# First layer of a four-layer trunk: shift and scale chunks in pairs, values in one pass over eight banks, the other modulation chunks dealt to attention, projection and FFN

## Chip, core and metric

One core of a Trainium2 chip runs the whole program once. The metric is the device time in microseconds, median of three runs.

## What is computed

```python
for li in range(DEPTH):                       # 4 layers: attention, retention, neighbourhood, attention
    sh1, sc1, gt1, sh2, sc2, gt2 = ada_mod(c, w_ada[li], b_ada[li])       # silu(c) @ w + b, 6 x 1024
    zsh1, zsc1, zgt1, zsh2, zsc2, zgt2 = ada_mod(cz, w_ada[li], b_ada[li])
    hx = modulate(x, norm_g[li, 0], sh1, sc1) # rms_norm(x, g) * (1 + scale) + shift
    hz = modulate(z, norm_g[li, 0], zsh1, zsc1)
    ox, oz = mixer(hx, hz, ...)               # layer 0: differential attention, 8 heads
    x = x + gt1 * ox
    x = x + gt2 * swiglu(modulate(x, norm_g[li, 1], sh2, sc2), ffn_in[li], ffn_out[li])
    # the same for z (the context) with its own modulation
return rms_norm(x, final_g)
```

x and ctx have 256 tokens of 1024 features each, all in f32. The FFN's hidden width is 2816.

## The kernel before

Features lie on the partitions: xT is 8 tiles (m or k) of 128 x 512 tokens, the first 256 columns x (stream 0), the others the context (stream 1). Each product of the layers is three matmuls of fp32r parts (h_hi w_hi, h_lo w_hi, h_hi w_lo). The weights are 424 blocks of 128x1024, called units; unit c goes through a ring of four slots: SyncE (SP) loads it to w_raw, ScalarE rounds it to w_hi (`conv`, in two halves), GpSimd subtracts to w_lo (two halves, `lo_ready`), TensorE uses it and counts `unit_used`. Each engine has one queue in program order, written out by hand; semaphores join them.

Modulation of a layer is 48 chunks of 128x1024 (shift 1, scale 1, gate 1, shift 2, scale 2, gate 2, eight each). For each chunk VectorE makes two products, one for each stream, with the conditioning vector: one SCALAR_TENSOR_TENSOR with an accumulated sum each (`ada_product`, L1452). `ada_sums` (L1460) adds the bias, `modulation` (L1492) makes the amplitude gain*(1+scale). `ada_done` counts finished chunks.

Layer 0 computes all its 48 chunks itself, with the conditioning in SBUF (cond_0): chunks 0 to 15 (`ada_first_group`, groups of four loaded as 2 MB) ahead of the first norm, 16 to 47 (`ada_rest_groups`) in `values`, between and behind the copies of the value product. Layers 1 to 3 have theirs computed in the FFN of the layer before, with the conditioning in PSUM (cond_p, in the high banks): 40 chunks in the loop over the hidden tiles, 8 behind it, from a ring of two chunks (ada_raw). TensorE starts the second half of the FFN output, which writes the high banks, when `ada_done` has all of them.

The norm: ScalarE squares x, VectorE adds the squares to ssum (`add_square`, L1520), TensorE multiplies with ones (`square_sum`), ScalarE makes rstd (`root`). For each tile VectorE scales (`scaled`, L1542), ScalarE adds the shift and rounds (`high`, h_hi), VectorE makes the rest (`low_part`, L1550, h_lo, counts `h_ready`). In layer 0 stream 0 is normalised wholly, then stream 1. The value product has 8 units, 4 token blocks and 2 feature halves; `values` runs over half 0 in banks 0 to 3, then over half 1 in banks 6, 7, 4, 5, and reads the second four units for half 1.

Attention has 8 tiles (one head pair each). In tile t TensorE makes q (bank 6) and k (bank 7), turns and weights tile t-1, then makes the scores of tile t. VectorE's queue of a tile: `weights_(t-1)`, rotate q (L1689), rotate k, two maxima (L1711), `subnorm(t-1)` (L1748), four maxima, `low(t-1)` (L1754). `project`: units 24 to 31; for tiles 0 to 4 VectorE adds the residual (L1501), ScalarE squares it (the conversion of the next unit stands ahead of each square in its queue), VectorE adds the square. Tiles 5 to 7 are done for x first, then for the context, which waits for the x residual of tile 5 (`x_new`).

## Time and profile before

| | us |
|---|---|
| median of 3 runs (2588.33 to 2590.04) | 2589.16 |
| profiled execution | 2592.92 |
| its span | 2591.1 |
| TensorE busy | 2421.3 |
| VectorE busy | 1289.2 |
| GpSimd busy | 1118.2 |
| ScalarE busy | 970.4 |

Times in the rows are microseconds from the start of the span. The page cuts the span in 40 slices of 64.8 us; a 9 is 90% busy or more. A timeline row gives the start, the length, the engine, the line, what is written and read, how many instructions it merges, and in brackets the idle time before it and the instruction that ended that.

### The profile page before, as it was taken

How to read it: one execution, taken by the hardware profiler on the slowest of the kernel's cores; microseconds unless marked ns; L12 is line 12 of the kernel's file. 1: busy time of each engine (PE TensorE's matmuls, PEld its weight loads, DVE VectorE, ACT ScalarE, POOL GpSimd, SP SyncE). 2: the span in 40 equal slices, each digit the busy share in tenths (PEclk: the TensorE clock that was granted, in tenths of full speed). 3: DMA queues.
4: the chain of work that ended last, by engine and by line, in shares of the span. 5: the costliest groups of instructions: out<-in, count | busy, mean ns of one | idle time of the engine just before them, and what ended most of it. 6: DMA issues, size and time to landing. Idle time of an engine off the chain costs nothing.

```text
span 2591.1 us, 37198 instructions
## 1 busy us (share of the span) xinstructions
PE 2421.3 (93%) x12212; PEld 1992.5 (77%) x12212; DVE 1289.2 (50%) x2275; ACT 970.4 (37%) x1943; POOL 1118.2 (43%) x855
## 2 busy tenths in 40 slices
PE   0729999999999999999999999999999999998998
PEld 0516678888887777788888887777888888777998
DVE  7996657654423333226666314554766443475211
ACT  2205544333223333323333224554432323455563
POOL 2321234444543433343544545223444554434896
PEclk9969999999999999999999999999999999999999
DMA  7256124554433222233655433231555442323554
GB/s 299 106 186 98 50 65 173 201 193 163 154 90 94 81 67 70 73 97 116 217 194 178 170 90 106 74 84 54 174 201 192 163 154 90 103 68 98 170 182 135
DMA packets 116466, 341.64 MB, mean 132 GB/s; under 512 B 34977, under 2 KB 36257, under 8 KB 115745
## 3 DMA queue, kind: packets, MB, share of 16 engines
q1 hardware_dynamic: 108352, 335.01, 39.4%
q10 hardware_dynamic: 8032, 5.52, 1.5%
q8 instruction: 55, 0.90, 0.1%
q14 instruction: 27, 0.21, 0.0%
HBM read 335.80 MB, written 4.69 MB: 131 GB/s over the span
## 4 chain that ended last, share of the span: by engine, by line
issue 60%; POOL 22%; PE 16%; DVE 1%; POOLq 1%; ACT 1%; DMA 0%; DVEq 0%; ACTq 0%; SPq 0%
POOL w_lo L492 22%; PE low_banks L499 15%; PE high_banks L499 1%; POOLq L491 0%; DVE tmp L1542 0%; POOLq L486 0%; DVE h_lo L1550 0%; ACT w_hi L1038 0%; DMA w_raw<-in_weights 0%; DMA ret_exp<-in_ret_exp 0%; DVE ssum_rstd L1452 0%; DVE xT L2028 0%; ACT lnm L1062 0%; POOLq L207 0%; ACT ssum_rstd L1063 0%
## 5 line engine op out<-in xcount | busy, mean ns | idle before, releaser
L492 POOL TENSOR_TENSOR w_lo<-w_raw,w_hi 128x512 fp32r<-128x512 f32 x848 | 1117.7, 1345 | 1454.2 <-ACT w_hi L1038 1453.5
L1038 ACT ACTIVATE w_hi<-w_raw 128x512 fp32r<-128x512 f32 x848 | 483.5, 624 | 474.1 <-PE low_banks L499 223.9
L499 PE MATMUL low_banks<-h_hi,w_hi 128*128 128x512 f32 (+1 forms) x1792 | 643.6, 359 | 14.8 <-POOL w_lo L492 7.7
L499 PE MATMUL low_banks<-h_lo,w_hi 128*128 128x512 f32 (+1 forms) x1792 | 634.5, 354 | 0.0
L499 PE MATMUL low_banks<-h_hi,w_lo 128*128 128x512 f32 (+1 forms) x1792 | 634.2, 354 | 0.0
L499 PEld LDWEIGHTS low_banks<-h_hi,w_hi 128*128 128x128 f32 x1792 | 340.5, 190 | 70.9 <-issue 11.3
L499 PEld LDWEIGHTS low_banks<-h_lo,w_hi 128*128 128x128 f32 x1792 | 340.7, 190 | 47.6 <-issue 1.9
L499 PEld LDWEIGHTS low_banks<-h_hi,w_lo 128*128 128x128 f32 x1792 | 340.6, 190 | 46.4
L1452 DVE SCALAR_TENSOR_TENSOR ssum_rstd<-ada_raw,high_banks 128x1024 f32<-128x1024 f32 x288 | 351.2, 1220 | 44.6 <-DMA ada_raw<-in_ada_w 36.9
L1360 ACT ACTIVATE lnm<-low_banks 128x512 f32<-128x512 f32 (+1 forms) x88 | 47.8, 544 | 427.3 <-PE low_banks L499 427.2
L1929 DVE TENSOR_TENSOR tmp<-low_banks,lnm 128x512 f32<-128x512 f32 (+1 forms) x88 | 55.0, 625 | 284.9 <-ACT lnm L1360 281.2
L499 PE MATMUL high_banks<-h_hi,w_hi 128*128 128x512 f32 (+1 forms) x384 | 148.4, 387 | 14.1 <-ACT v_all L1146 14.1
L499 PE MATMUL high_banks<-h_lo,w_hi 128*128 128x512 f32 (+1 forms) x384 | 144.5, 376 | 0.0
L499 PE MATMUL high_banks<-h_hi,w_lo 128*128 128x512 f32 (+1 forms) x384 | 144.4, 376 | 0.0
L499 PE MATMUL high_banks<-u_hi,w_hi 128*128 128x256 f32 (+1 forms) x424 | 141.0, 332 | 0.5 <-POOL w_lo L492 0.5
L499 PE MATMUL high_banks<-u_lo,w_hi 128*128 128x256 f32 (+1 forms) x424 | 140.3, 331 | 0.0
L499 PE MATMUL high_banks<-u_hi,w_lo 128*128 128x256 f32 (+1 forms) x424 | 140.3, 331 | 0.0
L499 PE MATMUL low_banks<-u_hi,w_hi 128*128 (+2 forms) x352 | 127.6, 362 | 0.0
L499 PE MATMUL low_banks<-u_lo,w_hi 128*128 (+2 forms) x352 | 127.6, 362 | 0.0
L499 PE MATMUL low_banks<-u_hi,w_lo 128*128 (+2 forms) x352 | 127.6, 362 | 0.0
L1501 DVE SCALAR_TENSOR_TENSOR xT<-high_banks,mod,xT 128x256 f32<-128x256 f32 x52 | 24.6, 479 | 177.0 <-PE high_banks L499 177.0
L499 PEld LDWEIGHTS high_banks<-h_hi,w_hi 128*128 128x128 f32 x384 | 73.6, 192 | 41.4 <-ACT v_all L1146 14.6
(195 smaller groups left out, 3687.9 us busy)
## 6 DMA issues: line engine op xcount, KB each, us to landing
w_raw<-in_weights SPq DMA_DIRECT2D x424, 512.0 KB, 3.7
ada_raw<-in_ada_w SPq DMA_DIRECT2D x144, 512.0 KB, 3.9
ada_rest<-in_ada_w SPq DMA_DIRECT2D x8, 2048.0 KB, 8.2
ada_first<-in_ada_w SPq DMA_DIRECT2D x4, 2048.0 KB, 14.5
bias<-rpb_skew SPq DMA_DIRECT2D x64, 64.0 KB, 2.5
rpb_skew<-rpb_rows ACTq DMA_DIRECT2D x1, 3556.0 KB, 34.8
cond_l<-in_cond SPq DMA_DIRECT2D x3, 1024.0 KB, 4.7
xT<-in_xT SPq DMA_DIRECT2D x1, 2048.0 KB, 14.4
```

What stands on the lines that cost most here:

```text
L492: nc.gpsimd.tensor_tensor(out=w_lo[:, r, part], in0=w_raw[:, r, part], in1=w_hi[:, r, part], op=ALU.subtract).then_inc(lo_ready, 1)
L499: return nc.tensor.matmul(dst, lhsT, rhs, start=start, stop=stop, **kw)
L1038: nc.scalar.activation(w_hi[:, r, part], w_raw[:, r, part], ACT.Copy).then_inc(hi_ready, 1)
L1360: nc.scalar.activation(lnm[:, 0:L.W], bank[2 * s][:, 0:L.W], ACT.Silu)\
L1452: last = V.scalar_tensor_tensor(out=dump, in0=w, scalar=1.0, in1=cond[:, c, :], op0=ALU.mult, op1=ALU.mult, accum_out=ada_sum[:, r, c:c + 1])
L1501: return V.scalar_tensor_tensor(out=x, in0=src[:, COLS[c]], scalar=gate_of(L, which, m, c), in1=x, op0=ALU.mult, op1=ALU.add)
L1929: V.tensor_tensor(out=tmp[:, s, 0:L.W], in0=bank[2 * s + 1][:, 0:L.W], in1=lnm[:, 0:L.W], op=ALU.mult).then_inc(L.u_free, 1)
```

## The change

**Start.** The first 16 chunks come as single 0.5 MB loads in pairs (shift m, scale m) in the order of tiles (`ada_pair`), with x in two halves and the first units between them; the small tables go to ScalarE's DMA queue. TensorE sums the squares tile by tile in PSUM (`first_square_sum`); VectorE adds none. VectorE makes the four products of pair m, the bias and the amplitude of that one tile, scales both streams, and puts the low parts of tile m-1 behind the first product of pair m (`first_pair`, `first_values`). The value product runs once over the tiles k, all 8 accumulations in 8 banks at a time; the units come in the order 0, 4, 1, 5, ... (`first_unit_of`).

**Chunks 16 to 39** (48 products) are dealt by `rest_products`: 10 around the value copies and in tile 0, three in each of tiles 1 to 6, two in tile 7 (ADA_TILE), 18 in the projection (ADA_PROJECT). Their loads go to slots that have come free (ADA_GROUPS), behind waits on SP. **Chunks 40 to 47** go to the FFN of layer 0, which now makes 56: 40 in the loop and 16 behind it, two loads behind each weight load.

```diff
+ADA_GROUPS = ((16, 0, (0, 4, 16, 17, 18, 1, 5)), (23, 1, (2, 6, 3, 7)), (27, 0, (3,)), (28, 1, (7,)), (29, 0, (3,)),
+              (30, 1, (7,)), (31, 0, (8, 9, 10, 11)), (35, 1, (13, 14, 15, 16, 17)))
+ADA_MIXER = 40
+ADA_TILE = ((2, 2, 2, 4), (1, 1, 1), (1, 1, 1), (1, 1, 1), (1, 1, 1), (1, 1, 1), (1, 1, 1), (1, 1, 0))
+ADA_PROJECT = (7, 3, 3, 3, 2)
...
@@ SP @@
+            sp.wait_ge(ada_done, 30)
+            sp.wait_ge(plan[0].vst_ready, KT)
             ada_rest_load(6)
+            sp.wait_ge(ada_done, 31)
+            sp.wait_ge(plan[0].t_done, KT * plan[0].groups)
             ada_rest_load(7)
...
-                    for k in range(ADA_LAST):
+                    per = ada_last(L.li) // 8
+                    for k in range(8):
                         loads(at)
-                        ada_load(L.li + 1, r + k, 0, 0)
+                        for j in range(per):
+                            ada_load(L.li, r + k * per + j, 0, 0)
                         at += 1
@@ TensorE @@
+            def first_values(L):
+                for k in range(KT):
+                    s = k // 2
+                    if k % 2 == 0:
+                        first(2 * s + 1)
+                    else:
+                        take(2 * s + 1)
+                    for c in range(2):
+                        pe.wait_ge(h_ready[c], k + 1)
+                        for half in (1, 0):
+                            for tb in (2 * c, 2 * c + 1):
+                                last = three(bank[V_BANKS[half][tb]][:, :],
+                                             tuple(t[:, k, tb * P:tb * P + P] for t in H),
+                                             weight(2 * s + half, k % 2 * 512, k % 2 * 512 + 512), k == 0, k == KT - 1)
...
+            def first_square_sum():
+                for m in range(KT):
+                    pe.wait_ge(sq_ready[0], m + 1)
+                    for c in range(2):
+                        last = mm(bank[MS_BANKS[0][c]][:, COLS[c]], ones[:, :], tmp[:, m % 2, COLS[c]], m == 0, m == KT - 1)
...
@@ ScalarE @@
+            def first_values(L):
+                for m in range(KT):
+                    high(0, L, m, 0)
+                    high(0, L, m, 1)
+                    if m in (2, 4, 6):
+                        conv(AHEAD + m - 2)
+                        conv(AHEAD + m - 1)
...
                     if place:
+                        if L.li == 0 and place == 1:
+                            act.wait_ge(ada_done, 21)
                         exps(t - 1, range(1 if place >= 2 else 0, L.banks))
                         value_rows(t - 1)
-                    elif L.li == 0:
-                        act.wait_ge(mod_ready, 2)
...
-            for c in range(AHEAD):
-                conv(c)
+            conv(0)
             root(0, 0)
             root(0, 1)
+            for c in range(1, AHEAD):
+                conv(c)
@@ VectorE @@
+            def first_values(L):
...
+                for m in range(KT):
+                    first_pair(m, lambda: low_parts(m - 1))
+                    for c in range(2):
+                        if m == 0:
+                            dve.wait_ge(rstd_ready[c], 1)
+                        scaled(0, L, m, c)
+                low_parts(KT - 1)
+                constants()
+                rest_products(ADA_TILE[0][0])
...
                     if place:
+                        rest_products(extra[0])
                         weights_(t - 1)
...
                     rotate(bank[6][:, 0:SEQ], qT[:, 0:SEQ], 0).then_inc(L.qk_dve, 1)
+                    rest_products(extra[1])
                     dve.wait_ge(L.qk_act, t * (1 + L.zq) + (1 + L.zq))
                     dve.wait_ge(L.qk_dve, t * 2 + 1)
                     rotate(bank[7][:, 0:SEQ], kT[:, 0:SEQ], 2).then_inc(L.qk_dve, 1)
+                    rest_products(extra[2])
                     maxima(t, 0, range(2))
...
+                    if L.li == 0:
+                        rest_products(ADA_PROJECT[0])
                     for m in range(L.first):
                         dve.wait_ge(unit_used, n + m + 1)
                         residual(L, 2, bank[out_bank(L, m)], m, L.W)
                         if m < KT - 1:
                             add_square(e0 + m + 1, m % 2, L.W)
+                        if L.li == 0 and m < 4:
+                            rest_products(ADA_PROJECT[m + 1])
+                    if L.li == 0:
+                        own(amplitudes(0, 1))
```

What the order of instructions shows at the two places of which the prediction speaks most. First VectorE, ahead of the first norm. Before, from the last product of chunk 15 into the first tiles (L1452 is a product, L1542 scales, L1550 makes h_lo):

```order
L1452 SCALAR_TENSOR_TENSOR dump,ada_sum<-ada_first,cond 128x1024 [waits dve_own]
L1460 TENSOR_TENSOR mod<-ada_sum,bias_ada 128x8 [waits ada_done]
L1492 SCALAR_TENSOR_TENSOR amp<-mod,gain 128x16 [waits ada_done,dve_own]
L1536 MEMSET ssum_rstd 128x256 [waits x_rstd_ready,mod_ready]
L1542 SCALAR_TENSOR_TENSOR tmp<-xT,amp,ssum_rstd 128x256 [waits dve_own]
L1542 SCALAR_TENSOR_TENSOR tmp<-xT,amp,ssum_rstd 128x256
L1550 SCALAR_TENSOR_TENSOR h_lo<-tmp,mod,h_hi 128x256 [waits x_h_hi_ready]
L1542 SCALAR_TENSOR_TENSOR tmp<-xT,amp,ssum_rstd 128x256 [waits x_h_ready]
```

All 32 products stand above the first scaling, and stream 0 goes on tile after tile. In the change, one turn of the loop over pairs (L1575 is a product, L1587 the bias, L1589 the amplitude, L1676 scales, L1684 makes h_lo):

```order
L1575 SCALAR_TENSOR_TENSOR dump,ada_sum<-ada_first,cond 128x1024 [waits pair_loaded1]
L1684 SCALAR_TENSOR_TENSOR h_lo<-tmp,mod,h_hi 128x256 [waits x_h_hi_ready,dve_own]
L1684 SCALAR_TENSOR_TENSOR h_lo<-tmp,mod,h_hi 128x256 [waits z_h_hi_ready]
L1575 SCALAR_TENSOR_TENSOR dump,ada_sum<-ada_first,cond 128x1024
L1575 SCALAR_TENSOR_TENSOR dump,ada_sum<-ada_first,cond 128x1024 [waits ada_done]
L1575 SCALAR_TENSOR_TENSOR dump,ada_sum<-ada_first,cond 128x1024 [waits dve_own]
L1587 TENSOR_TENSOR mod<-ada_sum,bias_ada 128x2x2 [waits ada_done]
L1589 SCALAR_TENSOR_TENSOR amp<-mod,gain 128x2 [waits dve_own]
L1676 SCALAR_TENSOR_TENSOR tmp<-xT,amp,ssum_rstd 128x256 [waits dve_own]
L1676 SCALAR_TENSOR_TENSOR tmp<-xT,amp,ssum_rstd 128x256
```

The scaling of a tile now follows the four products of its own pair, both streams side by side, and the low parts of the tile before stand behind the first product.

Second VectorE, from the last low part of attention into the projection. Before (L1754 is the low part, L1501 a residual, L1520 the sum of squares):

```order
L1754 TENSOR_TENSOR y_lo<-tmp,y_hi 128x512 [waits y_hi_ready_0]
L1501 SCALAR_TENSOR_TENSOR xT<-high_banks,mod,xT 128x256 [waits unit_used]
L1501 SCALAR_TENSOR_TENSOR xT<-high_banks,mod,xT 128x256
L1520 TENSOR_TENSOR ssum_rstd<-ssum_rstd,tmp 128x512 [waits x_ssum_step,x_sq_ready]
L1501 SCALAR_TENSOR_TENSOR xT<-high_banks,mod,xT 128x256 [waits unit_used]
```

The first residual follows at once. In the change (L1905, L1635 and L1654 are the same three, L1605 is a product, L1563 adds the bias; the rows left out are five more products):

```order
L1905 TENSOR_TENSOR y_lo<-tmp,y_hi 128x512 [waits y_hi_ready_0]
L1605 SCALAR_TENSOR_TENSOR dump,ada_sum<-ada_first,cond 128x1024 [waits rest_loaded0]
L1605 SCALAR_TENSOR_TENSOR dump,ada_sum<-ada_first,cond 128x1024 [waits dve_own]
...
L1605 SCALAR_TENSOR_TENSOR dump,ada_sum<-ada_first,cond 128x1024 [waits ada_done]
L1635 SCALAR_TENSOR_TENSOR xT<-high_banks,mod,xT 128x256 [waits unit_used,dve_own]
L1635 SCALAR_TENSOR_TENSOR xT<-high_banks,mod,xT 128x256
L1654 TENSOR_TENSOR ssum_rstd<-ssum_rstd,tmp 128x512 [waits x_ssum_step,x_sq_ready]
L1605 SCALAR_TENSOR_TENSOR dump,ada_sum<-ada_first,cond 128x1024
L1563 TENSOR_TENSOR mod<-ada_sum,bias_ada 128x8 [waits ada_done]
L1605 SCALAR_TENSOR_TENSOR dump,ada_sum<-ada_rest,cond 128x1024 [waits rest_loaded1,dve_own]
L1605 SCALAR_TENSOR_TENSOR dump,ada_sum<-ada_rest,cond 128x1024 [waits dve_own]
L1635 SCALAR_TENSOR_TENSOR xT<-high_banks,mod,xT 128x256 [waits unit_used,ada_done]
```

Seven products stand ahead of the first residual, and three behind its square.

## Rows read from the trace of the kernel before

**Rows 1.** The page's busy row of TensorE, tenths in 40 slices of the span
```profile
PE   0729999999999999999999999999999999998998
```

**Rows 2.** Waits of 0 to 400 us: total, times, longest us
```profile
PE low_banks L499 <- DVE kT L1693: 39.7, 1, 39.7
PE low_banks L499 <- DVE h_lo L1550: 38.6, 1, 38.6
...
PE low_banks L499 <- DVE ssum_rstd L1520: 31.4, 1, 31.4
```

**Rows 3.** Busy us by stretch: PE, PEld, DVE, ACT, POOL; clock, DMA share, GB/s
```profile
20.00:40.00 20.00, 2.05 (x4) 1.17 (x4) 18.89 (x30) 6.68 (x12) 2.85 (x2) 1.00 1.03 410
160.00:180.00 20.00, 0.00 (x0) 0.00 (x0) 19.38 (x35) 0.00 (x0) 0.00 (x0) 0.50 0.71 274
```

**Rows 4.** Timeline of ScalarE: start us, us, what, idle before and its releaser
```profile
19.45 1.15 ACT L1054 ACTIVATE tmp<-xT 128x512 f32<-128x512 f32 x2 [9.35 <-DMA xT<-in_xT]
```

**Rows 5.** Timeline of VectorE, 0 to 75 us
```profile
15.90 1.22 DVE L1452 SCALAR_TENSOR_TENSOR dump<-ada_first,cond 128x1024 f32<-128x1024 f32 x1
...
39.68 2.16 DVE L1452 SCALAR_TENSOR_TENSOR dump<-ada_first,cond 128x1024 f32<-128x1024 f32 x1
...
69.73 0.17 DVE L1492 SCALAR_TENSOR_TENSOR amp<-mod,gain 128x16 f32<-128x16 f32 x1
...
72.83 0.48 DVE L1542 SCALAR_TENSOR_TENSOR tmp<-xT,amp,ssum_rstd 128x256 f32<-128x256 f32 x1
73.24 0.48 DVE L1550 SCALAR_TENSOR_TENSOR h_lo<-tmp,mod,h_hi 128x256 fp32r<-128x256 f32 x1
```

**Rows 6.** Timeline of TensorE, 0 to 704 us
```profile
32.36 1.06 PE L499 MATMUL high_banks<-ssum_rstd,ones 128*128 128x256 f32 x2
...
79.56 0.39 PE L499 MATMUL low_banks<-w_hi,h_hi 128*128 128x512 f32 x1
79.79 0.39 PE L499 MATMUL low_banks<-w_lo,h_hi 128*128 128x512 f32 x1
...
193.47 3.78 PE L499 MATMUL low_banks<-kT,qT 64*128 64x512 f32 x6 [39.72 <-DVE kT L1693]
...
702.70 0.39 PE L499 MATMUL high_banks<-u_hi,w_hi 128*128 128x512 f32 x1
```

**Rows 7.** Timeline of GpSimd, 0 to 400 us
```profile
37.16 15.85 POOL L492 TENSOR_TENSOR w_lo<-w_raw,w_hi 128x512 fp32r<-128x512 f32 x8 [36.14 <-ACT w_hi L1038]
...
278.79 4.95 POOL L492 TENSOR_TENSOR w_lo<-w_raw,w_hi 128x512 fp32r<-128x512 f32 x4 [15.63 <-ACT w_hi L1038]
...
370.96 14.91 POOL L492 TENSOR_TENSOR w_lo<-w_raw,w_hi 128x512 fp32r<-128x512 f32 x10 [25.46 <-ACT w_hi L1038]
```

**Rows 8.** Timeline of VectorE in a tile of attention
```profile
268.45 0.20 DVE L1724 RECIPROCAL d_st<-d_st 128x8 f32<-128x8 f32 x1 [1.63 <-ACT e_x L1163]
...
276.60 1.72 DVE L1689 TENSOR_TENSOR rot<-high_banks,da_rope 32x256 f32<-32x256 f32 x4 [1.31 <-ACT kT L1239]
...
281.21 1.29 DVE L1711 TENSOR_REDUCE d_st<-low_banks 128x1 f32<-128x512 f32 x2 [1.96 <-PE low_banks L499]
```

**Rows 9.** Timeline of VectorE from attention's end through the projection
```profile
366.79 0.75 DVE L1748 SCALAR_TENSOR_TENSOR tmp<-high_banks,subln,ssum_rstd 128x512 f32<-128x512 f32 x1 [11.79 <-ACT ssum_rstd L1063]
368.24 0.69 DVE L1754 TENSOR_TENSOR y_lo<-tmp,y_hi 128x512 fp32r<-128x512 f32 x1 [0.70 <-ACT y_hi L1210]
370.19 0.88 DVE L1501 SCALAR_TENSOR_TENSOR xT<-high_banks,mod,xT 128x256 f32<-128x256 f32 x2 [1.26 <-PE high_banks L499]
...
374.29 1.47 DVE L1520 TENSOR_TENSOR ssum_rstd<-ssum_rstd,tmp 128x512 f32<-128x512 f32 x1 [0.70 <-ACT tmp L1054]
...
384.63 0.47 DVE L1501 SCALAR_TENSOR_TENSOR xT<-low_banks,mod,xT 128x256 f32<-128x256 f32 x1
```

**Rows 10.** Timeline of VectorE behind the hidden part of FFN 0
```profile
649.81 1.22 DVE L1452 SCALAR_TENSOR_TENSOR ssum_rstd<-ada_raw,high_banks 128x1024 f32<-128x1024 f32 x1
```

**Rows 11.** The chunks of FFN 0 by tile: time from issue to landing
```profile
DMA to landing us min/median/max: 3.7/4.7/5.5
```

301 lines of the change are left out of this document (185 added, 116 removed).

## The prediction

> **What bounds the kernel now.** I read the page's busy row first: TensorE stands at 9 in nearly every slice and only the first three are thin [rows 1]. So the kernel is a chain of matmuls from about 200 us on, and a change can pay only where TensorE waits. The waits of the first 400 us name the places: 31.4 us until the sum of squares, 38.6 us until the first normalised tile (h_lo), and 39.7 us until the first rotated keys (kT) [rows 2]. All three are waits for VectorE, and the VectorE timeline shows why: it works through 96 modulation products of 128x1024 (48 chunks, two streams) [rows 5] before the scores of tile 0 start at 193.47 us [rows 6]. The forecast is what the new order makes of these 193 us, and what the products cost in the places they are dealt to. The profiled execution took 2592.92 us, 3.8 above the median of 2589.16; I sum against the execution and take the difference off the median.
>
> **Prices.** A product takes 1.22 us, 1.27 from start to start, while GpSimd rests, and 2.16 (2.2 start to start) while it splits weights [rows 5]. A split of half a unit takes 1.24 us alone (4 in 4.95) and 1.98 beside products (8 in 15.85) [rows 7]; in that stretch eight splits made seven products 0.94 us longer and one sum of chunks too, together about 8.4 us, so **one split overlapped by products costs VectorE 1.05 us**. A matmul of 512 columns comes every 0.23 us at the full clock [rows 6], a unit or one value tile (24 of them) every 5.45. A scaling and a low part take 0.91 us together [rows 5].
>
> **Part 1, up to the first normalised tile.** Before x (2 MB), 1 MB of conditioning and 2 MB of chunks were asked for; now 1 MB and 1 MB. x landed at 19.45 us [rows 4]; the loads run at 410 GB/s [rows 3], so 1 MB less is 2.4 us: its second half is there at about 17, the first at about 14.5. TensorE now sums the squares itself, 2 matmuls of 256 columns a tile, about 1 us each at the start [rows 6]: 2 us a tile for some 5 us, then about 1.1 if the clock rises. That gives the sums at 26 and, with the roots, both rstd at **28 us** (32 if the clock stays low; 24 if the loads are quicker). VectorE has ended pair 0 by 17 and waits.
>
> **Part 2, eight pairs with the value products.** Each further tile costs VectorE 4 x 1.27 (products) + 0.45 (sum, amplitude) + 2 x 0.91 (scalings, low parts) = 7.33 us, seven times 51.3. ScalarE converts three units before it makes the first h_hi, and units 4 to 9 in the loop; that is 18 splits, 18.9 us by the price above, and about 1.3 us of waiting for the first h_hi. The last scaling comes at 28 + 51.3 + 18.9 + 1.3 = 99.5 us and the last h_lo at 101. TensorE needs 5.45 us a tile, less than the 7.3 to 11.5 that VectorE gives it, so it follows; its last tile takes 5.5 to 7 (more, if it has fallen to the 1.2 GHz level, 0.50 of the clock, as it had in the wait of 40 us [rows 3]). **Values end at about 107.5 us.** With no splits in the way it would be 89, with all 18 at 1.05 and the half clock on every tile about 115.
>
> What the trace shows of the shared resource is a slowdown of both sides, 0.94 us for the product and 0.74 for the split [rows 5, 7]. The Trainium skill, SBUF — State Buffer, section Who interferes with whom, says that a VectorE instruction with two SBUF inputs and a GpSimd one that reads SBUF exclude each other for a whole instruction. By that rule each split would cost the products its own 1.24 us, 3.4 us more over the 18; the trace is nearer to the smaller figure.
>
> **Part 3, from the values to the scores of tile 0.** VectorE's last copy ends at 108.5. Then four products (5.1, and 4.2 for the four splits of units 10 and 11), the q rotation 2.7, two products and a sum 2.7, the k rotation 2.7: scores at about **126.5 us**. TensorE is done with q and k at 118.4, so 8 us of this is bare. Without splits it is 122, with the products at 2.2 throughout 130. Against 193.47 the gain is **67 us** (61 to 75).
>
> **Part 4, the other tiles of attention.** Three products go into each of tiles 1 to 6 and two into tile 7. VectorE had three gaps in a tile: 1.63 us until the last exponential, 1.31 until ScalarE's copy of k, 1.96 until the first scores [rows 8]. The first two take 1.27 with GpSimd resting. The third is beside splits (278.79 on [rows 7]) and takes 2.16: it ends 0.3 to 0.4 us late, but the next thing after the two maxima waits for rstd anyway. I charge **1 us** for all seven tiles; bounds 0 and, if every one of the 20 were bare at 1.27 to 2.2, 25 to 44 us (a rival below). The loads for them are asked for a tile ahead.
>
> **Part 5, the projection.** Here 18 products stand between the residuals, and this is the one place where cover is missing. The 11.8 us in which VectorE idles lie before the last low part of attention; the products come after it. From that low part (368.24) to the residual of tile 5 (384.63) VectorE took 16.4 us [rows 9], a step of 2.95 per tile. Added now: 18 x 1.27 = 22.9, three sums and the amplitudes 0.9, and contention. GpSimd split ten halves in this stretch [rows 7], and VectorE's additions already paid about 3 us for it; I take 9 us on the products less those 3. That is 29.8 us, less the 1.3 that VectorE idled ahead of residual 0 [rows 9]: 28.5. Queued behind the waiting VectorE are ScalarE's squares, and behind each square the conversion of the next unit: units 29, 30 and 31 arrive 4 to 5 us apart too late, but TensorE has all three done while VectorE is still in its fourth round, so these stalls lie inside the big one. TensorE then waits for x_new of tile 5. Before, the halves of tiles 6 and 7 held the sum of squares back by some 2 us; now they don't, though TensorE may start again at the lower clock. **Cost 28 us** (23 without any contention, 33 with each product at 2.2).
>
> **Part 6, FFN of layer 0.** 56 chunks in place of 48; the extra 8 follow the hidden part. The ring holds two chunks, so two chunks take a landing (4.7 us [rows 11]) and a product pair (2.55), 7.35 with the handover. The second chunk was done at 651.0 [rows 10]; seven more rounds end at 702.5. TensorE waits for all chunks before the second half of the output, which began at 702.70 [rows 6]. A draw; **1 us**, bounds 0 and 5 (landings at 5.5 us). SP holds the weight loads behind these chunks: 8 rounds at 7.35 and not 5.44 us lag 15 us at the end. A load is asked for four units (21.8 us) ahead of its conversion, and the conversion stands three units (16 us) ahead of its use; less landing, conversion and splits some 25 us of that is spare. No charge, 3 us in the range.
>
> **Sum.** 67 - 1 - 28 - 1 = 37 us: 2592.9 becomes 2556, the median 2589.2 becomes **2552 us**.
>
> **Rivals.**
> (a) *Projection half covered*, 2539 us: if ScalarE and TensorE were what set the pace there, the products would fill VectorE's waits and cost about 15. For it: 0.70 us of idle time for each square. Against: the rows show no other pauses than these and the 1.26 at the front, 5 us in all up to the residual of tile 5, and the ones for squares stay [rows 9]. Chance 0.12.
> (b) *The first layer is later*, 2567: values end at 118 to 123, because TensorE keeps falling back to 1.2 GHz between tiles and conversions, which wait for used units, hold up h_hi. For it: while it waited in the values stage now, the clock did stand at 0.50 [rows 3]. Against: even at 10.9 us a tile TensorE hardly lags VectorE. Chance 0.17. A smaller form of it is slow loads. The Trainium skill, DMA: Bandwidth & Descriptors, section Bandwidth, wants DMAs of at least 1 MiB for three quarters of the peak, and the change cuts 2 MB chunk loads to 0.5 MB. In the trace the loads of 0.5 and 2 MB together run at 410 GB/s [rows 3]. By the page's figure for 1 MB, 341 GB/s, the 4.5 MB up to x would take some 2 us longer, an estimate.
> (c) *Slower: the tile's chain takes the products.* If each of the 20 products of tiles 1 to 7 delays weights, keys or scores by its full time beside splits, 2.2 us, that is 44 us; the sum is 67 - 44 - 28 - 1 = -6, so 2595. It turns slower from 1.9 us a product. Against: the three gaps [rows 8]. Chance 0.04.
> (d) *The FFN ring starves TensorE*, 2562: the weight loads of the last round come 10 us too late. Against: the spare time of part 6. Chance 0.04.
> (e) Nothing of note, because the waits move to something the trace does not show: 0.02.
>
> **How the numbers follow.** The forecast has 0.61. Its own range by parts 1 to 6 is 2541 to 2563; with (a) and (b) mostly in, 2534 to 2569. What this kernel's timing can tell from no change is about 0.2%, 5 us. Faster by more than that 0.94, within 0.02, slower 0.04.
>
> **What would show it.** In the new trace: first h_lo near 31 us and TensorE in eight bursts from there; pairs of about 7.3 us where GpSimd rests and up to 12 where it works; values ended at 105 to 110; scores of tile 0 at 126.5; from there to the last low part of attention 176 us, as now (193.5 to 368.9); then seven products, and 46 us from that low part to the residual of tile 5 with TensorE waiting for it; no wait over 3 us at the second half of the FFN output. A tile of attention above 21.5 us, or a projection under 35 us, would prove parts 4 or 5 wrong.

## Result, and the profile after

The changed kernel takes 2551.11 us (median of 4 runs, 2550.18 to 2553.03) against 2589.07 for the kernel before in the same session: a ratio of 0.985 (interval 0.984 to 0.987), 38 us less. The forecast was 2552. The profiled execution took 2551.37 us with a span of 2549.6, where that of before had a span of 2591.1.

TensorE's busy row shows where it came from. The first three slices stood at 0, 7 and 2 [rows 1] and are 4, 6 and 9:

```profile
PE   4699979999999999999999999999999999998998
```

A 7 has come in the sixth slice, 319 to 382 us: the projection. The waits of the first 400 us name both. In place of the three long ones of [rows 2] stand (total, times, longest us):

```profile
PE high_banks L542 <- DVE h_lo L1684: 25.0, 6, 7.4
PE low_banks L542 <- ACT tmp L1134: 21.1, 1, 21.1
...
DVE lnm L2140 <- DMA ident<-in_ident: 18.8, 1, 18.8
...
PE low_banks L542 <- DVE xT L1635: 10.0, 1, 10.0
...
PE low_banks L542 <- DVE kT L1844: 7.8, 1, 7.8
```

The wait for the sum of squares has become one of 21.1 us for the first square, and ahead of it stands something the forecast did not have: VectorE's own first instruction waits 18.8 us for a small table (ident). The 38.6 us for h_lo are now 25.0 in six pieces, the 39.7 for kT are 7.8, and the wait for xT, 10.0 us, is new.

Five instants divide the way to the second norm. This table has them for all kernels, in us from the start of the span: the first scaling of the first norm on VectorE, the scores of tile 0 on TensorE, the last low part of attention, and the reset of the sum of squares behind the projection, when rstd of the second norm is there. The last column is the median less that of the kernel before in the same session.

| kernel | first scaling | scores of tile 0 | last low part | reset | median | less before |
|---|---|---|---|---|---|---|
| before | 70.33 | 193.47 | 368.24 | 391.57 | 2589.07 | |
| changed | 32.33 | 128.16 | 302.47 | 352.88 | 2551.11 | -38.0 |
| a1_after_again | 31.17 | 128.17 | 303.04 | 353.71 | 2552.95 | -37.3 |
| e1_order | 25.42 | 120.91 | 295.14 | 345.41 | 2545.43 | -44.7 |
| e2_gap | 31.16 | 128.22 | 303.26 | 343.94 | 2543.16 | -47.0 |
| e3_both | 25.53 | 121.16 | 295.47 | 336.46 | 2535.97 | -54.0 |
| e4_project_narrow | 30.75 | 126.51 | 300.06 | 331.47 | 2533.95 | -56.2 |
| e5_tiles_narrow | 32.06 | 127.89 | 302.24 | 352.60 | 2554.05 | -36.1 |
| e6_no_splits | 30.70 | 104.12 | 276.18 | 326.84 | 2528.68 | -61.3 |
| e7_ring | 32.19 | 128.06 | 302.42 | 352.78 | 2570.68 | -19.3 |
| e8_four | 25.80 | 121.48 | 316.54 | 346.59 | 2548.83 | -41.4 |

Of the first two rows: the scores come 65.3 us earlier; attention takes 174.3 us where it took 174.8, 0.5 less (no gain can be read from that: a1_after_again, the same kernel, takes 174.9); from its last low part to the reset it takes 50.4 where it took 23.3, a loss of 27.1. That is 38.7 us at the reset. The spans differ by 41.5; the other 2.8 us lie behind the reset, 2.7 of them behind layer 0 (the residual that follows the second half of the FFN output stands at 748.57 before and 709.80 now), where nothing is changed: the profiled execution of before was 3.8 us above its median, and this is probably most of it.

### The profile page after: what moved, and what is told of

It reads as the page before. It is cut to its first block, busy times and chain, and to the rows that moved or that the text cites. A ratio compares the mean times of both kernels' runs of the same rounds, so it can differ in the third digit from the quotient of the medians.

```text
span 2549.6 us, 37152 instructions
## 1 busy us (share of the span) xinstructions
PE 2436.9 (96%) x12240; PEld 2005.0 (79%) x12240; DVE 1295.2 (51%) x2280; ACT 969.0 (38%) x1944; POOL 1123.5 (44%) x855
## 4 chain that ended last, share of the span: by engine, by line
issue 59%; POOL 25%; PE 11%; DVE 2%; POOLq 1%; ACT 1%; DMA 1%; DVEq 0%; ACTq 0%; SPq 0%
POOL w_lo L535 25%; PE low_banks L542 11%; PE high_banks L542 1%; DVE tmp L1676 0%; DVE dump L1575 0%; POOLq L534 0%; DVE h_lo L1684 0%; POOLq L529 0%; ACT w_hi L1118 0%; DMA w_raw<-in_weights 0%; DMA ada_raw<-in_ada_w 0%; DMA ret_exp<-in_ret_exp 0%; DVE xT L2189 0%; ACT h_hi L1154 0%; ACT lnm L1142 0%
## 5 line engine op out<-in xcount | busy, mean ns | idle before, releaser
L1555 DVE SCALAR_TENSOR_TENSOR ssum_rstd<-ada_raw,high_banks 128x1024 f32<-128x1024 f32 x304 | 370.7, 1220 | 46.8 <-DMA ada_raw<-in_ada_w 38.5
L542 PE MATMUL high_banks<-w_hi,h_hi 128*128 128x512 f32 x224 | 89.9, 401 | 27.5 <-DVE h_lo L1684 25.0
L1635 DVE SCALAR_TENSOR_TENSOR xT<-high_banks,mod,xT 128x256 f32<-128x256 f32 x52 | 24.6, 479 | 173.4 <-PE high_banks L542 173.3
## 6 DMA issues: line engine op xcount, KB each, us to landing
xT<-in_xT SPq DMA_DIRECT2D x2, 1024.0 KB, 12.1
```

The lines of the kernel that those rows point to most:

```text
L542: return nc.tensor.matmul(dst, lhsT, rhs, start=start, stop=stop, **kw)
L1555: last = V.scalar_tensor_tensor(out=dump, in0=w, scalar=1.0, in1=cond[:, c, :], op0=ALU.mult, op1=ALU.mult, accum_out=ada_sum[:, r, c:c + 1])
L1635: return V.scalar_tensor_tensor(out=x, in0=src[:, COLS[c]], scalar=gate_of(L, which, m, c), in1=x, op0=ALU.mult, op1=ALU.add)
```

## The first layer, as it runs now

VectorE, at the start and through the second and third turn of the loop over pairs (L1575 product, L1684 low part, L1676 scaling), a timeline like [rows 5]:

```profile
18.79 0.42 DVE L2140 TENSOR_TENSOR lnm<-ssum_rstd 128x256 f32<-128x256 f32 x1 [18.79 <-DMA ident<-in_ident]
...
32.33 2.85 DVE L1676 SCALAR_TENSOR_TENSOR tmp<-xT,amp,ssum_rstd 128x256 f32<-128x256 f32 x2 [7.04 <-ACT ssum_rstd L1143]
...
46.34 0.88 DVE L1676 SCALAR_TENSOR_TENSOR tmp<-xT,amp,ssum_rstd 128x256 f32<-128x256 f32 x2
...
53.38 0.88 DVE L1676 SCALAR_TENSOR_TENSOR tmp<-xT,amp,ssum_rstd 128x256 f32<-128x256 f32 x2
54.18 1.22 DVE L1575 SCALAR_TENSOR_TENSOR dump<-ada_first,cond 128x1024 f32<-128x1024 f32 x1
55.44 1.91 DVE L1684 SCALAR_TENSOR_TENSOR h_lo<-tmp,mod,h_hi 128x256 fp32r<-128x256 f32 x2
57.28 2.30 DVE L1575 SCALAR_TENSOR_TENSOR dump<-ada_first,cond 128x1024 f32<-128x1024 f32 x1
...
61.86 2.16 DVE L1575 SCALAR_TENSOR_TENSOR dump<-ada_first,cond 128x1024 f32<-128x1024 f32 x1
...
64.45 0.88 DVE L1676 SCALAR_TENSOR_TENSOR tmp<-xT,amp,ssum_rstd 128x256 f32<-128x256 f32 x2
...
100.44 0.88 DVE L1676 SCALAR_TENSOR_TENSOR tmp<-xT,amp,ssum_rstd 128x256 f32<-128x256 f32 x2
```

The turn from 46.34 to 53.38 takes 7.04 us, the next 11.07. What the second has and the first has not is GpSimd, which splits four halves in it (the first turn of all, 32.33 to 46.34, has most splits, seven with the one under way at its start, and takes 14.0 us, longer than the 12 that the forecast allowed):

```profile
55.54 7.39 POOL L535 TENSOR_TENSOR w_lo<-w_raw,w_hi 128x512 fp32r<-128x512 f32 x4 [11.99 <-ACT w_hi L1118]
```

TensorE follows, as forecast: in the loop it waits for h_lo and VectorE never for it. The windows of the changed kernel (busy us and counts of PE, PEld, DVE, ACT, POOL; clock, DMA share, GB/s) show the loads of the start and the pair loop in two parts:

```profile
20.00:32.00 12.00, 10.48 (x32) 7.87 (x32) 5.12 (x10) 6.79 (x14) 1.03 (x1) 1.00 1.03 410
32.00:70.00 38.00, 22.47 (x79) 17.37 (x80) 36.94 (x53) 9.83 (x21) 18.77 (x12) 0.80 0.77 295
70.00:109.00 39.00, 29.96 (x114) 23.72 (x113) 37.07 (x64) 10.03 (x20) 13.76 (x8) 0.89 0.22 71
```

VectorE is busy for 36.94 of 38.00 us and 37.07 of 39.00: the loop is VectorE's. The granted clock in it is a mean of 0.80 and 0.89, so TensorE does fall to its lower level around the bursts (matmuls 0.43 us apart in place of 0.23), and it costs little, since it waits anyway; only in the last burst do VectorE's copies wait for it, 0.45 and 0.67 us.

## Experiments

All are made from the changed kernel. a1_after_again is that kernel itself, to have it beside others in one session.

> The changed kernel once more, with nothing altered, beside the other kernels on the same chip: 2551 us, with the first scaling at 31 to 32.5 us. In the runs so far the first scaling came anywhere from 30.7 to 32.3 us with the same code ahead of it, since the landing of the last small table sets it; if the small tables do set the start, this run will show the same spread, and all that follows will move with it up to the scores of tile 0.

2552.95 us, 37.3 less than before. The first scaling did stand elsewhere, at 31.17, but the scores of tile 0 at 128.17 as in the first trace (128.16): the 1.2 us were lost again on the way. The trace tells where: the last h_lo is still 1.1 us early (100.40 against 101.50), but TensorE then takes 8.4 us and not 7.3 for the last tile of the values, at a granted clock of 0.68 and not 0.77 (102 to 109.5 us), and the last copy stands at 109.49 where it stood at 109.48. So the last part of the expectation was wrong. Differences of a microsecond in the start are not to be read.

### What the start waits for: e1_order

```diff
-            act.wait_ge(lam_sums, 1)
-            ...exponentials of the small tables...
             for m in range(KT):
                 ...
                 square(KT, m, TOK, m % 2)
+            act.wait_ge(lam_sums, 1)
+            ...exponentials of the small tables...
@@ VectorE, first_pair @@
                 ...the four products of the pair...
+                if m == 0:
+                    small_tables()     # waits for small_in; was ahead of the loop
                 parts = mod[:, 0, :, :]...
```

> The changed kernel, with two stretches of code in another order: ScalarE squares the eight tiles of x before it takes the exponentials of the small tables, and VectorE makes the products of pair 0 before it waits for the small tables. In the trace of the changed kernel the last small table (ident) lands at 18.8 us, VectorE's first instruction stands at 18.79 and the first square at 20.31, while the two halves of x had landed at about 13.3 and 15.8. Theory A, the start waits for the small tables: the first square comes at 13 to 14 us, TensorE's sums end at about 25 instead of 31.5, the first scaling at 25 to 26 instead of 32.33, and all that follows moves with it: 2544 to 2546 us, 5.5 to 7 less than 2551.1. Theory B, the loads set the pace (weights and pairs come too late for an earlier start): the first scaling is earlier, but VectorE waits for the loads of pairs 2 to 7 later, and less than 2 us is left of it: 2549 to 2551.

The median is 2545.43, 44.7 less than before where the changed kernel is 37.3 to 38.0 less: 7 us. Theory A holds, at each of its points. (The run moves both waits for the small tables, ScalarE's and VectorE's; it does not part them.) ScalarE in e1_order:

```profile
13.02 1.15 ACT L1134 ACTIVATE tmp<-xT 128x512 f32<-128x512 f32 x2 [2.29 <-issue]
...
22.31 0.63 ACT L1134 ACTIVATE tmp<-xT 128x512 f32<-128x512 f32 x1 [0.40 <-PE high_banks L542]
```

and VectorE:

```profile
14.12 1.23 DVE L1585 SCALAR_TENSOR_TENSOR dump<-ada_first,cond 128x1024 f32<-128x1024 f32 x1
18.57 0.43 DVE L1571 TENSOR_TENSOR lnm<-ssum_rstd 128x256 f32<-128x256 f32 x1 [3.21 <-DMA ident<-in_ident]
...
25.42 2.85 DVE L1688 SCALAR_TENSOR_TENSOR tmp<-xT,amp,ssum_rstd 128x256 f32<-128x256 f32 x2 [5.43 <-ACT ssum_rstd L1143]
```

x is there at 13 us, the tables at 18.6 as before. From the first scaling to the scores it is 95.5 us (95.8 in the changed kernel): the earlier start is kept whole, and no load comes too late for it.

### What the products of the projection cost: e4_project_narrow and e2_gap

e4 makes the 18 products there over 8 columns:

```diff
-                        rest_products(ADA_PROJECT[0])
+                        rest_products(ADA_PROJECT[0], 8)
...
-                            rest_products(ADA_PROJECT[m + 1])
+                            rest_products(ADA_PROJECT[m + 1], 8)
```

> The changed kernel, with the 18 products of the projection made over 8 columns in place of 1024 (so chunks 31 to 39 of the modulation, and the output, are not those of the reference). It measures what they cost. Theory A, nearly bare, as forecast: from the last low part of attention to the last sum of squares the stretch goes from 47.6 to about 21 to 24 us (before 21.1), with some 3 us left for 18 short instructions and their sums; 2525 to 2529 us in all, 24 to 27 less. Theory B, half covered: 12 to 15 us less, 2536 to 2539.

The stretch falls from 50.4 to 31.4 us, by 19.0, and the median by 18 to 19. (The 47.6 and 21.1 us of the expectation are the same stretch up to the last sum of squares, 3 us ahead of the reset.) That is neither theory: too much for half cover, and 8 us more than nothing is left where 3 were expected. The first full round of VectorE in e4 tells why:

```profile
302.12 0.88 DVE L1635 SCALAR_TENSOR_TENSOR xT<-high_banks,mod,xT 128x256 f32<-128x256 f32 x2
303.77 0.85 DVE L1654 TENSOR_TENSOR ssum_rstd<-ssum_rstd,tmp 128x512 f32<-128x512 f32 x1 [0.77 <-ACT tmp L1134]
304.55 1.25 DVE L1605 SCALAR_TENSOR_TENSOR dump<-ada_first,cond 128x8 f32<-128x8 f32 x1
...
305.84 1.21 DVE L1563 TENSOR_TENSOR mod<-ada_sum,bias_ada 128x8 f32<-128x8 f32 x1
307.08 1.21 DVE L1605 SCALAR_TENSOR_TENSOR dump<-ada_rest,cond 128x8 f32<-128x8 f32 x1
...
308.34 0.17 DVE L1605 SCALAR_TENSOR_TENSOR dump<-ada_rest,cond 128x8 f32<-128x8 f32 x1
```

A product of 8 columns takes 0.17 us alone, and 1.21 to 1.25 where GpSimd splits (it does from 302.77 to 308.27). It did 1/128 of the work and lost the same 1.05 us as a whole product. So the two engines do not slow each other down in proportion to their work: **an instruction of VectorE with both inputs in SBUF stands still until the running split is over** (the last one held up ends at 308.29, the splits at 308.27). GpSimd's side fits: a pair of splits takes 3.48 us beside whole products in the changed kernel, and 2.55 beside the short ones here. So the products' own work is the 19 us that went (18 times 1.27 less 0.21), and the splits' cost stayed. What is left above the kernel before is 8.1 us: nine short instructions stood still for 1.05 us each, 9.4, and 22 short ones (products, sums, the amplitude) take 4.6; off go 3.3 of contention and 1.3 of idle time that the stretch had before [rows 9], and 1.5 because the last tiles now wait less for TensorE, 7.9 in all.

e2 puts eight products into the gap of 11.85 us ahead of the last scaling:

```diff
+ADA_GAP = 8
-ADA_PROJECT = (7, 3, 3, 3, 2)
+ADA_PROJECT = (0, 3, 3, 3, 1)
...
                 weights_(KT - 1)
+                if L.li == 0:
+                    rest_products(ADA_GAP)
                 subnorm(KT - 1, LAST_O)
```

> The changed kernel, with 8 of the 18 products of the projection put into the 11.85 us in which VectorE idles ahead of the last scaling of attention (289.1 to 301.0 in its trace); none stands ahead of the first residual, and 3, 3, 3 and 1 between the residuals. Their four chunks come as two groups of two loads. Theory A, the products of the projection are bare and each gives back what it takes: the seven ahead of the first residual took 10.8 us there (303.07 to 313.83), the eighth 1.3; the gap holds eight at 1.27 with GpSimd resting, 10.2 us. From the last low part of attention to the last sum of squares 35 to 37 us instead of 47.6: 2539 to 2541 us in all. Theory B, half of them is covered by what ScalarE and TensorE do there: it falls by 5 us or less, 2546 us. Theory C, the loads land behind the start of the gap and push the last scaling from 301.0 to 304 or later: 2543 us.

2543.16, 47.0 less than before: 9 to 10 us better than the changed kernel, where A said 10 to 12 and B 5. The stretch from low part to reset takes 40.7 instead of 50.4 (37.9 to the last sum of squares, where A said 35 to 37). The time is the one that C gave, but not C's reason: the first load is 1.3 us late, and yet the last scaling of attention starts at 301.81, not at 304. The gap, in e2:

```profile
291.21 1.22 DVE L1607 SCALAR_TENSOR_TENSOR dump<-ada_first,cond 128x1024 f32<-128x1024 f32 x1 [1.29 <-DMA ada_first<-in_ada_w]
...
300.27 1.22 DVE L1607 SCALAR_TENSOR_TENSOR dump<-ada_first,cond 128x1024 f32<-128x1024 f32 x1
...
301.81 0.75 DVE L1901 SCALAR_TENSOR_TENSOR tmp<-high_banks,subln,ssum_rstd 128x512 f32<-128x512 f32 x1
```

Eight products at 1.22, the first 1.29 us late because its load was, and the scaling no longer waits for anything: the gap is full, and from the scores of tile 0 it takes 175.0 us to the low part instead of 174.3. The saving is 9.7, about what eight products take alone (10.2), and not the 12.1 that the eight took, for the same reason as in e4. In the changed kernel two of the seven products ahead of the first residual took 2.19; in e2 none stands there, and the splits meet the next three instead:

```profile
307.66 2.31 DVE L1607 SCALAR_TENSOR_TENSOR dump<-ada_rest,cond 128x1024 f32<-128x1024 f32 x1
...
312.25 2.18 DVE L1607 SCALAR_TENSOR_TENSOR dump<-ada_rest,cond 128x1024 f32<-128x1024 f32 x1
```

### The tiles of attention: e5_tiles_narrow

```diff
-                        rest_products(extra[0])
+                        rest_products(extra[0], 8)
...
-                    rest_products(extra[1])
+                    rest_products(extra[1], 8 if place else D)
-                    rest_products(extra[2])
+                    rest_products(extra[2], 8 if place else D)
```

> The changed kernel, with the 20 products in tiles 1 to 7 of attention made over 8 columns in place of 1024 (so chunks 21 to 30 of the modulation, and the output, are not those of the reference). Theory A, VectorE's gaps cover them: the tile keeps its period of 20.55 us, and from the scores of tile 0 to the last low part of attention it takes 173.5 to 174.3 us, as with them; 2550 to 2551 us in all. Theory B, the chain of the tile takes them: at 1.27 to 2.2 us a product the stretch would be 25 to 44 us shorter, 2507 to 2526. Between the two, 0.3 us a tile for the product beside GpSimd's splits would give 2 us, 2549.

174.35 us from the scores to the low part, against 174.31 and 174.87 (a1_after_again) with the products in full, and TensorE's tiles 20.57 us apart in both. The 20 products cost nothing there: theory A. (The median is 36.1 us below before, not 37.3 to 38.0; up to the reset the two traces agree within 0.3 us, so this is not from the tiles.)

### What the splits take from the pair loop: e6_no_splits

```diff
-            with pool.Fori(0, UN // RING) as i:
+            for c in range(12):
+                for j, part in enumerate(HALVES):
+                    part = slice(part.start, part.start + 8)
+                    ...the same wait and subtraction, 8 columns...
+            with pool.Fori(0, UN // RING - 3) as k:
+                i = k + 3
```

> The changed kernel, with GpSimd's splits of units 0 to 11 made over 8 columns in place of 512 (w_lo of these units is otherwise zero, so the output is not the reference's). It takes away what VectorE's products run against in the first layer's pairs and ahead of the scores of tile 0. Theory A, each split of the loop costs VectorE about 1.05 us: from the first scaling to that of pair 7 it takes 51 to 53 us (seven turns of 7.3) instead of 68.1, TensorE's values end at about 93 to 96 instead of 109.4, and with the four contended products behind them at 1.22 the scores of tile 0 come at 108 to 110 instead of 128.2; in all 18 to 20 us less, 2531 to 2533. Theory B, GpSimd has no part in it and the pairs are long because ScalarE makes the conversions ahead of h_hi: the loop shrinks by under 5 us and the products stay at 2.2 us, 2546 or more. Theory C, with VectorE faster TensorE becomes the bound of the values, at 0.50 of its clock: values at 10.9 us a tile, ending at 115 or later, so nothing is gained.

The loop of e6 goes through six turns of 7.04 to 7.11 us after its first:

```profile
30.70 0.48 DVE L1685 SCALAR_TENSOR_TENSOR tmp<-xT,amp,ssum_rstd 128x256 f32<-128x256 f32 x1 [5.73 <-ACT ssum_rstd L1152]
...
40.00 0.88 DVE L1685 SCALAR_TENSOR_TENSOR tmp<-xT,amp,ssum_rstd 128x256 f32<-128x256 f32 x2
...
47.05 0.88 DVE L1685 SCALAR_TENSOR_TENSOR tmp<-xT,amp,ssum_rstd 128x256 f32<-128x256 f32 x2
...
82.42 0.88 DVE L1685 SCALAR_TENSOR_TENSOR tmp<-xT,amp,ssum_rstd 128x256 f32<-128x256 f32 x2
```

51.7 us instead of 68.1, 16.4 less for 18 splits: 0.91 us each, or 0.86 if the one that was under way at 32.33 is counted too (a split of 8 columns still holds VectorE up by a few hundredths here and there, 1.26 for 1.22). From the last scaling to the scores it is 21.7 instead of 27.7 us, 6 less: 4.7 of them behind the last copy of the values, where five instructions of VectorE stand beside splits in the changed kernel (four products at 2.17 to 2.19 us, a sum at 1.10) and none in e6; and 1.3 ahead of it, where the last tile of the values had taken TensorE 7.3 us at a clock of 0.76 and now takes 5.7 at 1.00. The median is 23 to 24 us below the changed kernel's, more than the 18 to 20 of A: its mechanism holds, but the values end at 89.8 us, where it had 93 to 96. B and C are out. Each of these splits costs VectorE, on the average of the loop, about three quarters of its own 1.24 us.

### The ring behind the hidden part: e7_ring

```diff
-ADA_TRIPS = ((10, 4), (1, 0))
+ADA_TRIPS = ((8, 4), (3, 0))
```

> The changed kernel, with the loop over the hidden tiles making 32 chunks and not 40, and 8 more behind it (24 in layer 0, 16 in layers 1 and 2, where there were 16 and 8). Theory A, behind the hidden part a chunk costs 3.7 us (a landing and two products for two chunks) and TensorE waits for the last of them before the second half of the output, with 6 us to spare in layer 0 now (last product ends at 657.9, the half begins at 663.8): 8 more chunks are 29.4 us, so TensorE waits about 23.5 us in layer 0. Layers 1 and 2 then stand where layer 0 stands now, with their 6 us to spare, and cost nothing: 2573 to 2577 us. Theory B, the loads then run freely and a chunk costs only its two products, 2.55 us: 8 chunks are 20.4, and the wait 14.5 us: 2565. Theory C, TensorE doesn't wait for the last chunk at all: 2551.

2570.68, 18 to 19 us more than the changed kernel (-19.3 against -37.3 and -38.0). The traces of the changed kernel and of e7_ring, last product behind the hidden part (VectorE), and in e7_ring the second half of the output (TensorE):

```profile
656.71 1.22 DVE L1555 SCALAR_TENSOR_TENSOR ssum_rstd<-ada_raw,high_banks 128x1024 f32<-128x1024 f32 x1
```

```profile
681.61 1.22 DVE L1555 SCALAR_TENSOR_TENSOR ssum_rstd<-ada_raw,high_banks 128x1024 f32<-128x1024 f32 x1
```

```profile
682.89 0.80 PE L542 MATMUL high_banks<-u_hi,w_hi 128*128 128x512 f32 x1 [12.06 <-DVE ssum_rstd L1555]
```

Eight chunks end 24.9 us later, 3.1 a chunk, and the half starts at 682.89 instead of 663.92: 19.0, that is 24.9 less the 6.0 to spare. A's mechanism holds, TensorE does wait for the last chunk and the spare time is 6 us; its price, 3.7 a chunk, was too high, since the loads land in 3.7 us at the median and not in the 4.7 of [rows 11]. The wait is shown as 12.06 and not 19 us because TensorE was 7 us late already (682.89 less 12.06 is 670.83). From 560 to 700 us ScalarE waited 63 us in all for the weight loads that stand behind the chunks on SP, and 16.4 in the changed kernel; TensorE then waited 3.5 us for w_lo (2.95 and 0.59), and behind the first of these waits 13 matmuls came 0.43 and not 0.23 us apart, 2.7 us more (granted clock 0.84 from 650 to 671 us; 1.00 in the changed kernel from 650 to 663.9). That is most of the 7. This is rival (d) of the forecast, now real:

```profile
ACT w_hi L1118 <- DMA w_raw<-in_weights: 63.1, 10, 9.3
```

### Both edits, and one too many: e3_both and e8_four

> The changed kernel with both edits together: the squares and the products of pair 0 ahead of the small tables, and 8 products in the gap ahead of the last scaling of attention. The two lie one behind the other on the path and share nothing, so the gains should add up: 6 and 11 us, 2533 to 2536 us. If the second hides behind the first (TensorE or the loads as a common bound) it is 2539 or more.

e3 is e1 and e2 together: 2535.97 us, a ratio to before of 0.979 (0.978 to 0.981), 16 us below the changed kernel and 54 below before. The gains add up: 7.0 us at the scores (121.16 against 128.16), and 9.4 in the stretch of the projection (41.0). It is the fastest kernel here that computes the whole.

e8 adds a fourth product to each of tiles 1 to 6, in VectorE's queue ahead of the scaling:

```diff
-ADA_TILE = ((2, 2, 2, 4), (1, 1, 1), (1, 1, 1), (1, 1, 1), (1, 1, 1), (1, 1, 1), (1, 1, 1), (1, 1, 0))
-ADA_PROJECT = (0, 3, 3, 3, 1)
+ADA_TILE = ((2, 2, 2, 4),) + 6 * ((1, 1, 1, 1),) + ((1, 1, 0, 0),)
+ADA_PROJECT = (0, 1, 1, 1, 1)
...
                     if place:
+                        rest_products(extra[3] if len(extra) > 3 else 0)
                         subnorm(t - 1, da_banks(L)[0])
```

> The kernel with both edits, and a fourth product in each of tiles 1 to 6 of attention, between the two first maxima and the scaling; the loads are dealt anew to the slots that are free. Four products are left in the projection where ten were. In the trace of the changed kernel VectorE still waits 1.88 us ahead of the maxima and 1.16 us ahead of the scaling, in each tile. Theory A, what these two waits hold is enough for a fourth product, beside a splitting GpSimd too: the tile keeps 20.57 us, and from the scores of tile 0 to the last low part it stays at 174.3 us; the projection loses six products at 1.27, and its splits still cost what they cost: from the last low part to the reset of the sum of squares 33 to 34 us instead of 41.0; 2528 to 2530 us in all. Theory B, the tile is full with three: the fourth makes each tile 1 to 2.2 us longer, 6 to 13 us, and takes back the 7 or more: 2535 to 2542.

2548.83, 12.6 us worse than e3. The projection does fall, to 30.1 us, but attention takes 195.1 instead of 174.3. B, and stronger than it said: a full tile is 24.2 us instead of 20.6. VectorE in e8:

```profile
213.90 1.72 DVE L1854 TENSOR_TENSOR rot<-high_banks,da_rope 32x256 f32<-32x256 f32 x4 [1.64 <-issue]
...
218.52 1.29 DVE L1876 TENSOR_REDUCE d_st<-low_banks 128x1 f32<-128x512 f32 x2
219.73 2.10 DVE L1619 SCALAR_TENSOR_TENSOR dump<-ada_first,cond 128x1024 f32<-128x1024 f32 x1
221.86 1.10 DVE L1565 TENSOR_TENSOR mod<-ada_sum,bias_ada 128x4 f32<-128x4 f32 x1
223.00 0.75 DVE L1913 SCALAR_TENSOR_TENSOR tmp<-low_banks,subln,ssum_rstd 128x512 f32<-128x512 f32 x1
```

The same place in the changed kernel:

```profile
236.04 1.29 DVE L1862 TENSOR_REDUCE d_st<-low_banks 128x1 f32<-128x512 f32 x2
238.42 0.75 DVE L1899 SCALAR_TENSOR_TENSOR tmp<-low_banks,subln,ssum_rstd 128x512 f32<-128x512 f32 x1 [1.09 <-ACT ssum_rstd L1143]
```

Between maxima and scaling lay 1.09 us of waiting, and that was all. The 1.88 us ahead of the maxima, on which the expectation counted too, stand in tile 7 alone, which has no third product; in tiles 1 to 6 the third had used them up, and I had read one tile for all. The fourth product took 2.10 beside the splits, and a sum of eight elements behind it another 1.10, as in e4; less 1.09, the scaling is 2.1 us late, and TensorE waits 2.29 us for it where it waited 0.20. The other 1.6 of the 3.7 us a tile come behind that wait, from TensorE's clock. These are the first 5.2 us of its q products in a tile of e8 and in one of the changed kernel (columns as in the windows above):

```profile
224.80:230.00 5.20, 5.20 (x17) 4.16 (x17) 4.57 (x11) 4.06 (x15) 0.00 (x0) 0.67 0.19 72
```

```profile
219.70:225.00 5.30, 5.30 (x24) 4.38 (x24) 4.67 (x12) 4.04 (x15) 0.00 (x0) 1.00 0.60 198
```

Behind the wait of 2.3 us some eight matmuls come 0.43 us apart, then 0.23 again; behind the wait of 0.20 they come 0.23 apart from the start. For q and k TensorE needs 12.8 us in place of 11.2, and that is the 1.6. The row at 213.90 is what VectorE sees of it: it waits 1.64 us ahead of the rotation of k, where it waits for nothing in the changed kernel. The trace names no releaser, but the rotation reads ScalarE's copy of k, which stands behind TensorE's k products and ends at 213.82:

```profile
213.43 0.39 ACT L1336 ACTIVATE kT<-high_banks 128x256 f32<-128x256 f32 x1 [5.06 <-PE high_banks L544]
```

So three products a tile is the most that this place holds; no run tries the fourth at another. This is rival (c) of the forecast, one product further on.

## Why the forecast was right, step by step

**Part 1, rstd at 28.** Wrong by 4 us, and in its cause. 28 was the time of the first scaling; it was 32.33. x was there earlier than forecast (its halves landed at 13.3 and 15.8 us, I had 14.5 and 17), but I had VectorE end pair 0 by 17, and it began it at 19.86. The step that failed is "the small tables go to ScalarE's DMA queue", which stands in the description of the change and had no price in the sum. Its last table landed 14.8 us after issue, where it was 3.5 on SP's queue ahead of the large loads, and ScalarE's squares stand behind two exponentials and a logarithm that need VectorE's first results. e1_order shows the cost: without this wait the first scaling comes at 25.4. Whether the other queue or the place behind the large loads made the tables late, no run tells: none puts them back on SP's queue.

**Part 2, values.** First scaling to last: 71.5 forecast (51.3, 18.9 and 1.3), 68.1 measured; the last scaling at 99.5 forecast, 100.44 measured. So the errors of parts 1 and 2 cancel, and the right time of this stage is in part luck. The turn was taken at 7.33 (its terms add up to 7.35) and is 7.04. The 18 splits were taken at 1.05, and e6 measures 0.91. The sum behind the 1.05 is wrong: seven products and one sum, each 0.94 us longer, are 7.5 us and not 8.4, so 0.94 a split and 16.9 us for the 18, 2 us less than the 18.9 charged. What failed besides is the reading of the shared resource. I took the 0.94 us that a product and the 0.74 that a split were longer [rows 5, 7] for a slowdown of both sides. e4_project_narrow shows that it is exclusion: an instruction of 0.17 us waits 1.0 to 1.1 us beside splits of 1.24. The trace of the kernel before had it already: that one sum of chunks lies among the eight splits of [rows 7] and takes 1.11 us, and a like one without a split beside it 0.17:

```profile
44.09 1.11 DVE L1460 TENSOR_TENSOR mod<-ada_sum,bias_ada 128x8 f32<-128x8 f32 x1
...
59.20 0.17 DVE L1460 TENSOR_TENSOR mod<-ada_sum,bias_ada 128x8 f32<-128x8 f32 x1
```

A slowdown in proportion would have made it 0.3. The Trainium skill, SBUF — State Buffer, section Who interferes with whom, says just this of a VectorE instruction with two SBUF inputs and a GpSimd one that reads SBUF, and that one with a single SBUF input, outside VectorE's 2-port modes, does not contend. The trace agrees in the second point too: in FFN 0, where the conditioning lies in PSUM, a product beside splits takes what it takes alone (changed kernel, GpSimd and VectorE):

```profile
651.36 2.54 POOL L535 TENSOR_TENSOR w_lo<-w_raw,w_hi 128x512 fp32r<-128x512 f32 x2 [3.92 <-ACT w_hi L1118]
```

```profile
651.88 1.22 DVE L1555 SCALAR_TENSOR_TENSOR ssum_rstd<-ada_raw,high_banks 128x1024 f32<-128x1024 f32 x1
```

Only the price is below the 1.24 that I had made of the rule: 0.91 a split in the loop, 0.94 to 1.1 for each instruction that is held up. Why the rest of a split costs nothing is not shown. For the sum of this change the difference was 3 us; for e4 and e2, whose expectations I made with a cost per product, it was the miss.

Rival (b), values ending at 118 to 123, did not come (109.4), though TensorE did fall back between its tiles; nor did its smaller form, slow loads: from 20 to 32 us loads of 0.5 MB alone run at 410 GB/s.

**Part 3.** Values ended at 109.4 (forecast 107.5), since the last tile took TensorE 7.3 us, at the long end of the 5.5 to 7 given; scores at 128.16 (forecast 126.5). The last copy ended at 110.2 (108.5); from there to the scores it took 18.0 us, as forecast, but with other terms: those of the forecast add up to 17.4 and held four splits, and five instructions met one. Gain 65.3 for 67.

**Part 4.** Charged 1 us, and nothing can be measured: 174.8 us before, 174.3 and 174.9 in two traces of the changed kernel, 174.35 without the products' work in e5. The three gaps of [rows 8] hold three products, and e8 shows that a fourth ahead of the scaling finds no room.

**Part 5.** 28 forecast, 27.1 measured; low part to the residual of tile 5 in 45.3 us (46), with TensorE waiting for it, 9.96 us:

```profile
348.29 0.58 PE L542 MATMUL low_banks<-y_hi,w_hi 128*128 128x256 f32 x1 [9.96 <-DVE xT L1635]
```

Rival (a), half covered, is refuted as it was put: 18 products at 8 columns give back 19.0 us, and e2's eight give back 9.7, 1.05 to 1.2 a product. But the forecast's other half, contention that belongs to the products, is refuted too: it belongs to the splits and stays.

**Part 6.** Charged 1 us, measured 0: from the reset to the first residual behind the second half it takes 357.0 us before and 356.9 now. The last product ends at 657.93, 6 us ahead of that half; forecast was a draw (702.5, moved up by the 38.7, is 663.8). The round of two chunks was taken at 7.35, and e7 measures 6.2. e7 also shows that the edge is real.

**The total**: 67 - 1 - 28 - 1 = 37 forecast; 65.3 + 0.5 - 27.1 - 0 = 38.7 by the traces, 38.0 by the medians. The three terms that matter hold each by itself; that the total is met to 1 us is luck, since the start came 4 us late and the pairs made up for 3 of them. The 65.3 us are read from the two traces; no run makes the new start alone.

## What to carry to other kernels

Before work is moved onto an engine, look for its idle time of the right length and put the work there: twenty products in gaps of 1.3 to 2 us cost nothing, eighteen in a stretch without gaps cost 1.05 to 1.5 us each, and eight of these were free as soon as they stood in front of a wait of 11.8 us. Count contention between VectorE and GpSimd, where both read SBUF as here, by the number of GpSimd instructions that fall into VectorE's busy time, not by the size or number of VectorE's. When a wait of TensorE grows, look at its granted clock behind it: in e7 and e8 the slower matmuls cost 2.7 and 1.6 us on top of 3.5 and 2.3 us of waiting. And when a change moves small loads to another queue, ask which first instruction waits for the last of them.

## What the runs showed of the hardware

- A VectorE instruction with both inputs in SBUF, started while GpSimd subtracts 128x512 from SBUF (1.24 us), ends 0.9 to 1.1 us late whatever its size: 128x1024 at 2.16 to 2.31 for 1.22, 128x8 at 1.18 to 1.27 for 0.17, a sum over 128x4 from 0.16 to 1.10. With one input in PSUM it isn't late (1.22).
- Seven small loads (1 to 256 KB) on ScalarE's queue, beside 0.5 MB and 1 MB loads on SP's (353 GB/s in all from 1 to 19 us), landed one after the other, 6.9 to 14.8 us from issue; on SP's queue, ahead of x and the chunks (kernel before), ident took 3.5 us. Size has little to do with it: the table of 256 KB, first in the queue, took 6.9 us, and one of 1 KB, sixth, 14.1.
- Loads of 0.5 MB from a ring of two landed in 3.7 us at the median behind the hidden part.
- TensorE's matmuls of 512 columns come 0.23 or 0.43 us apart, the clock's two levels. Behind waits of 1.34 and 1.90 us (pair loop of the changed kernel) and of 2.44 (a1_after_again) they came 0.23 apart at once, behind 2.30 (e8), 2.95 (e7) and 4.23 to 7.38 us (pair loop) 0.43 apart at first. So the length of the wait alone does not decide it.
